# The RWKV-7 mixing stage of a two-layer encoder: five elementwise steps go to GpSimd, and VectorE's modulation products change places

## The reference

```
kk = heads(k * k_k);  kk = kk / max(norm(kk), 1e-12)
k  = k * (1 + (a - 1) * k_a)
y  = scan over t:  S = S*w_t + (S(-kk_t))(kk_t*a_t) + v_t k_t;  y_t = S r_t      (32 heads of 64)
y  = (y - mean) * rsqrt(var + eps) * ln_w + ln_b
y  = (y + sum(r*k*r_k) * v) * g        # bonus, gate
out = y @ w_o
```

## Time and profile before

| | |
|---|---|
| median of three runs | 2628.8 us |
| profiled execution | 2628.9 us |
| its span | 2627.3 us |
| TensorE busy in the span | 2526.0 us (96%) |
| VectorE | 1899.0 us (72%) |
| ScalarE | 1253.8 us (48%) |
| GpSimd | 46.5 us (2%) |
| granted TensorE clock, mean | 0.987 |

### The profile page before, as it was taken

The page is one execution under the profiler, slowest core; times in us unless marked ns, Lnnn a source line. Parts: engine busy times, 40 slices in busy tenths (PEclk is TensorE's granted clock), DMA queues, the critical chain, the costliest instruction groups (busy, mean ns, idle before and its releaser), DMA issues.

```text
span 2627.3 us, 53443 instructions
## 1 busy us (share of the span) xinstructions
PE 2526.0 (96%) x20124; PEld 2223.5 (85%) x20124; DVE 1899.0 (72%) x2596; ACT 1253.8 (48%) x1926; POOL 46.5 (2%) x85
## 2 busy tenths in 40 slices
PE   7999997998899999999999999999999999999998
PEld 6888877888788888888888888888888888888887
DVE  6868757887687777777777776677887655555556
ACT  2245555666445444444444554344454444444445
POOL 2000020000000000000000000000000000000000
PEclk9999999999999999999999999999999999999999
DMA  9998893445568888888887678567688566656653
GB/s 401 416 319 310 288 336 118 145 142 182 192 232 273 285 295 282 285 287 285 283 286 266 218 237 285 186 218 244 236 295 286 195 191 190 189 190 191 189 166 133
DMA packets 442249, 640.28 MB, mean 244 GB/s; under 512 B 21920, under 2 KB 402976, under 8 KB 420256
## 3 DMA queue, kind: packets, MB, share of 16 engines
q1 hardware_dynamic: 438400, 626.35, 70.1%
q0 software_dynamic: 3744, 12.59, 1.2%
HBM read 624.18 MB, written 14.68 MB: 243 GB/s over the span
## 4 chain that ended last, share of the span: by engine, by line
PE 68%; DVE 4%; ACT 1%; issue 1%; DMA 0%; DVEq 0%; ACTq 0%; SPq 0%
PE ps L1813 44%; PE ps L1817 22%; DVE ada_ring L1859 1%; DVE wlo L1797 1%; ACT whi L1792 0%; PE ps L1444 0%; PE ps L1438 0%; DMA ada_ring<-in_ada 0%; DVE st L1345 0%; PE ps L1477 0%; PE ps L1835 0%; DVE nt L132 0%; DVE lgf L1342 0%; PE ps L1469 0%; PE ps L1459 0%
## 5 line engine op out<-in xcount | busy, mean ns | idle before, releaser
L1797 DVE TENSOR_TENSOR wlo<-raw,whi 128x1024 fp32r<-128x1024 f32 (+1 forms) x736 | 865.6, 1191 | 436.5 <-ACT whi L1792 435.1
L1813 PE MATMUL ps<-act,whi 128*128 128x512 f32 x3528 | 1095.4, 392 | 0.8 <-DVE act L145 0.8
L1792 ACT ACTIVATE whi<-raw 128x1024 fp32r<-128x1024 f32 (+1 forms) x736 | 745.7, 1030 | 634.6 <-PE ps L1817 628.1
L1817 PEld LDWEIGHTS ps<-act,wlo 128*128 128x128 f32 x3528 | 662.6, 188 | 145.9
L1817 PE MATMUL ps<-act,wlo 128*128 128x256 f32 x3528 | 696.2, 279 | 0.0
L1813 PE MATMUL ps<-hid,whi 128*128 128x512 f32 x2176 | 685.4, 396 | 8.1 <-DVE wlo L1797 7.1
L1813 PEld LDWEIGHTS ps<-act,whi 128*128 128x128 f32 x3528 | 534.9, 188 | 1.4 <-DVE wlo L1797 1.0
L1817 PEld LDWEIGHTS ps<-hid,wlo 128*128 128x128 f32 x2176 | 411.3, 189 | 92.4
L1817 PE MATMUL ps<-hid,wlo 128*128 128x256 f32 x2176 | 433.4, 280 | 0.0
L1813 PEld LDWEIGHTS ps<-hid,whi 128*128 128x128 f32 x2176 | 331.5, 189 | 11.0 <-DVE wlo L1797 4.6
L1859 DVE SCALAR_TENSOR_TENSOR ada_ring<-ada_ring,silu 128x2048 f32<-128x2048 f32 x128 | 292.5, 2285 | 12.8 <-DMA ada_ring<-in_ada 12.8
(11 more groups left out here) (276 smaller groups left out, 2118.4 us busy)
## 6 DMA issues: line engine op xcount, KB each, us to landing
raw<-in_f_w SPq DMA_DIRECT2D x480, 512.0 KB, 4.5
ada_ring<-in_ada SPq DMA_DIRECT2D x144, 1024.0 KB, 7.7
raw<-in_a_w_rkv SPq DMA_DIRECT2D x96, 512.0 KB, 7.7
raw<-in_b_w_in SPq DMA_DIRECT2D x56, 512.0 KB, 3.8
ada_ring<-in_ada SPq DMA_DIRECT2D x48, 512.0 KB, 5.1
raw<-in_f_w SPq DMA_DIRECT2D x64, 384.0 KB, 3.9
first_ring<-in_ada SPq DMA_DIRECT2D x16, 1024.0 KB, 12.7
raw<-in_a_w_o SPq DMA_DIRECT2D x32, 512.0 KB, 6.8
```

The costliest lines, as they stand in the source:

```text
L1792: self.nc.scalar.activation(self.whi[:, u % SPL, 0:n], self.raw[:, u, 0:n], ACT.Copy).then_inc(self.s("hi_ready"), 1)
L1797: self.nc.vector.tensor_tensor(self.wlo[:, u % SPL, 0:n], self.raw[:, u, 0:n], self.whi[:, u % SPL, 0:n].bitcast(F32), SUB).then_inc(self. ...
L1813: self.nc.tensor.matmul(self.ps[0:c1 - c0, banks[b], :], hi[:, kk, c0:c1], src[:, k].rearrange("p a t -> p (a t)"), start=k == 0, stop=False)
L1817: last = self.nc.tensor.matmul(self.ps[0:c1 - c0, banks[b], T:2 * T], lo[:, kk, c0:c1], src[:, k, 0, :], start=False, stop=k == ktotal - 1)
```

## The change

GpSimd gets a program of its own in this stage: for iterations 0 to 6 it does the normalisation's product, weight and bias, bonus, gate and the low part, ten instructions over 128 x 256 elements an iteration (VectorE had eight, with the weight and bonus, and the bias and gate, in one instruction each). Iteration 7 stays on VectorE, which first waits for GpSimd's last. On VectorE `normed`, `gated_in`, `gated` and `remainder` go. Half 1 moves from the last chunk of C to N, in front of P2 (where half 2 was); halves 2 and 3 stand in front of W32, where the two y steps were; half 4 stays between W32 and W64; half 5 moves from there into chunk 2 of C; half 0 of the next iteration moves from chunk 1 to chunk 3, and `ada_sums` from chunk 0 to chunk 3. The order of SyncE, ScalarE and TensorE is not changed.

```diff
@@ VectorE stage_N
-                adas(i, 2)
+                adas(i, 1)
                 grow(i, "P2", 3, ADD, "P1")
...
                 grow(i, "P4", 3, ADD, "P3")
-                if post:
-                    normed(i - 1)
-                    gated_in(i - 1, 1 - q)
+                adas(i, 2, 3)
                 grow(i, "W32", 1, SUB, "P4")
                 if prep:
                     prep_c(i + 1, 1 - q)
-                adas(i, 3, 4)
-                if i >= 2:
-                    remainder(i - 2)
-                adas(i, 5)
+                adas(i, 4)
                 grow(i, "W64", 3, SUB, "W32")
@@ VectorE stage_C, in the loop over c
                         if prep:
                             for j in range(2):
                                 prep_d(i + 1, j)
-                        ada_sums(i)
                     if c in (1, 2) and prep:
                         prep_e(i + 1, c - 1)
-                    if prep and c % 2:
-                        adas(i + 1, c // 2)
-                    if c == 2 and post:
-                        gated(i - 1)
+                    if c == 2:
+                        adas(i, 5)
+                    if c == 3:
+                        ada_sums(i)
+                        if prep:
+                            adas(i + 1, 0)
@@ VectorE, before and after the loop
-            adas(0, 0, 1)
+            adas(0, 0)
...
-            remainder(L - 2)
...
+            past(dve, L - 1, "yg")
+            past(dve, L - 1, "y_lo")
             normed(L - 1)
@@ GpSimd, new
+            def finish(i, q):
+                for j in range(2):
+                    at(pool, i, "rsv", j)
+                    tt("yn", b["y"][:], b["yc"][:], b["yr"][:], MUL)
+                for j in range(2):
+                    at(pool, i, "yn", j)
+                    nc.gpsimd.tensor_scalar(b["y"][:], b["y"][:], col(i, PV_LNW, j), col(i, PV_LNB, j), MUL, ADD).then_inc(s("yw"), 1)
+                for j in range(2):
+                    at(pool, i, "yw", j)
+                    at(pool, i, "bon", j)
+                    tt("yb", b["y"][:], b["y"][:], b["bon"][q][:], ADD)
+                for j in range(2):
+                    at(pool, i, "yb", j)
+                    pool.wait_ge(s(f"g_loaded{j}"), i * 16 + 16)
+                    tt("yg", b["yo"][:], b["y"][:], b["g"][:], MUL)
+                for j in range(2):
+                    at(pool, i, "y_hi", j)
+                    tt("y_lo", self.hid_lo[:, m, :], R[j]["yo"][:].unsqueeze(1), self.hid_hi[:, m, :].bitcast(F32), SUB)
+            for i in range(L - 1):
+                finish(i, i % 2)
```

More of the change, by code:

```diff
@@ L2628, in tensor, with gpsimd, tt, col @@
                 self.multiply(u, UK, UK * u, KT, COLS, ((0, P), (P, 2 * P)), self.hid, (0, 1)).then_inc(self.s("unit_used"), 1)
-        return Stage(sync, scalar, vector, tensor)
+        def gpsimd(pool):
+            def tt(name, out, a, b, op):
+                nc.gpsimd.tensor_tensor(out, a, b, op).then_inc(s(name), 1)
+            def col(i, first, j):
+                return self.pv[:, bass.ds(i * 2 + (first + j), 1)]
+            def finish(i, q):
+                for j in range(2):
+                    b = R[j]
+                    at(pool, i, "rsv", j)
+                    tt("yn", b["y"][:], b["yc"][:], b["yr"][:], MUL)
+                for j in range(2):
+                    b = R[j]
+                    at(pool, i, "yn", j)
+                    nc.gpsimd.tensor_scalar(b["y"][:], b["y"][:], col(i, PV_LNW, j), col(i, PV_LNB, j), MUL, ADD).then_inc(s("yw"), 1)
+                for j in range(2):
+                    b = R[j]
+                    at(pool, i, "yw", j)
+                    at(pool, i, "bon", j)
+                    tt("yb", b["y"][:], b["y"][:], b["bon"][q][:], ADD)
+                for j in range(2):
+                    b = R[j]
+                    at(pool, i, "yb", j)
[3 more added lines that the diff above has]
+                    at(pool, i, "y_hi", j)
+                    m = bass.ds(i * 2 + j, 1)
+                    tt("y_lo", self.hid_lo[:, m, :], R[j]["yo"][:].unsqueeze(1), self.hid_hi[:, m, :].bitcast(F32), SUB)
+            for i in range(L - 1):
+                finish(i, i % 2)
+        stage = Stage(sync, scalar, vector, tensor)
+        stage.has_pool, stage.pool = True, gpsimd
+        return stage
     def ffn(self, layer, pieces, following):
```

## The result

The changed kernel takes 2644.9 us, the median of four runs (2642.0 to 2649.7), against 2628.7 before: the ratio is 1.0069, with a 95% interval of 1.0057 to 1.0081. It is slower by 16 us, more than twice the 7 us of the forecast: inside the stated range of 2619 to 2647, and above the 2631 to 2641 of the forecast itself. A second session gave 2642.8 (six runs, 2635.8 to 2649.6), ratio 1.0056 (1.0041 to 1.0071).

A forecast was written before the change was run, and what follows sets the result against it. Neither VectorE nor TensorE was full, so the order of single instructions decides. Gain, late loads and GpSimd waits, -12.5 + 16.2 + 3.6 = +7.3 us on 2628.9, gave 2636 us, range 2619 to 2647.

The forecast's parts named there:

- The likeliest case: N of iterations 1 to 6: the slip by late `in` outweighs the gain, 2636 us; chance 0.43.
- The signs named beforehand: ScalarE waits 3 to 4 us an iteration for `in`, its loads stand in one row, VectorE idles before P2, W32 to W64 shrinks.
- third rival: GpSimd instructions each hold VectorE up once through SBUF and XE's delay is not covered: 2644 us; chance 0.13.
- The slip of N: Late loads of `in` delay DX4 to W32 by 2.7 us (1.2 to 4.7) in iterations 1 to 6: 16.2 us.
- a dip of the clock: TensorE's clock dips in front of DX4 in place of the old dip: 0, or 4 us gained if none comes.
- L - 2.3: Chain slip in N, L being the time from last issue of `in` to landing: taken as 5.0, between 3.5 and 7.0.
- The gain: W32 to W64 1.26, chunk 1 to 2 0.82, less 0.4 and 0.1 later in C: 1.6 us an iteration, 12.5 together.
- GpSimd in the way: Halves 2 and 3 wait for GpSimd in N, making W32 0.6 us late in six iterations: 3.6 us.
- first rival: Loads of `in` land in time, L near 3.5, N slips 1.2 us: about 2622 us, faster; chance 0.24.
- Loads in time: Loads of `in` land with L below 4, N slips 1.2 us: about 2622 us, faster; chance 0.24.
- Nothing to be measured: L about 4.2, low gain before W64, GpSimd at half price, no dips: sum 0, 2629 us; chance 0.2.
- The shared way into SBUF: GpSimd and VectorE exclude each other in N and at the end of C: 8 us more, 2644 us; chance 0.13.

The follow-up runs named there:

- e1_order: The changed kernel with SyncE issuing the four loads of `in` ahead of modulation half 2 of the next iteration: 2616.6 us, ratio 0.9958.
- e2_late: The kernel before, with SyncE waiting for VectorE's U of chunk 3 ahead of modulation half 2 and the loads of `in`: 2662.3 us, ratio 1.0122.
- e5_warm_short: The changed kernel with 10 further matmuls of 256 columns in TensorE's standstill in N of iterations 1 to 7: 2643.7 us, ratio 1.0067.
- e6_chunk0: The changed kernel with half 5 in chunk 0 of C, the two sums in chunk 1, SyncE's order unchanged: 2612.7 us, ratio 0.9946.
- e3_gpsimd: The changed kernel with VectorE's modulation halves and sums back in their old places, y steps still on GpSimd: 2619.2 us, ratio 0.9971.

## Why the prediction was right, and where its sizes were off

**The cause.** The likeliest case was the one that came: SyncE's unchanged order makes the loads of `in` wait for half 5, ScalarE's `prep_v` waits for them, DX2 and the whole of N behind it. e1_order takes this away and turns the loss into a gain, and e2_late puts it into the old kernel and gets the loss. The signs named beforehand are there too. The size is another matter: the time is 4 us above the forecast's own 2641 and lies at the third rival's 2644, whose mechanism was not at work. That it is still inside the range is owed to the range's taking in that rival.

**The term that was too small.** The slip of N was put at 2.7 us and a dip of the clock at nothing, as it would only replace the old one. Two things were off. The landing took 5.5 to 6.0 us (5.0 was taken), which by the forecast's own formula, L - 2.3, gives 3.2 to 3.7; and TensorE's first product behind DX2 did come 3.2 to 3.8 us later (7.64 after XE at 517.48, before 3.94). The wait itself was thus forecast as it came. In the iteration without a dip, W32 stands 19.76 us after XE (601.00), before 15.92, so that 3.8 us are the late loads and what follows from them. And the dip does not cost the same in its new place. Before, it made an iteration some 0.75 us longer; in N it adds some 2. There TensorE stands still for 3.0 to 3.6 us and not 1.9, the clock falls before it starts again and stays at 0.50 for nearly 7 us (516.2 to 522.9), where before it was half as long (526.3 to 529.7), and in that time TensorE makes the products for DX4 and P2 one after another. That this is why it costs more is argued, not tested. With a dip W32 stands 22.06 us after XE: together 6.1 us where 2.7 stood, in iterations 2 to 6. Iteration 1, also counted, slipped only 1.7, as its DX2 was late before too. By e1_order the whole term is 29 us over the stage and not 16.

**The gain.** The forecast had 12.5 us less 3.6 for GpSimd in the way, that is 8.9; e1_order, the change without late loads, gained 0.42%, 11 us. That the two are near is in part chance. W32 to W64 fell by 2.35 us, and 1.38 of them passed on to the U of chunk 1 (1.26 was taken), because ScalarE's `prep_norm` was next, as foretold. Chunk 1 to 2 gave 0.75 (0.82 was taken). Chunk 2 to 3 lost 0.61 (0.4), and from the last U to XE 0.53 were lost (0.1). That leaves 1.0 us an iteration and not 1.6: 32.38 fell to 31.33. The rest of the 11 us are the old dips, 0.7 to 1.0 us in each of four iterations; with e1_order they went, and the iterations from the third on have a clock of 1.00. In the first rival's sum, the numbers given make 2621 us and not 2622.

**GpSimd in the way.** In N 0.6 us were taken. In the iteration shown none came through: half 3 took 1.74 us in place of 1.21, but TensorE's product for W32 was later still, 4.0 us behind P4 as before, in e1_order too. It isn't always so: in the iteration without a dip above, and in e5_warm_short's, half 2 took 1.85 us, half 3 1.73, VectorE went on to W32 without idling, and it started 0.23 us late. It did come through at the end of C, where nothing had been counted because `in` would be late: the two sums took 0.40 and 0.66 us beside the low parts (0.15 and 0.16 in e6_chunk0, away from them), and XE came 2.43 us after U in place of 1.90, in e1_order too. The price of a GpSimd instruction was right: 0.71 us alone (0.75 was taken), the weight and bias 0.56.

The Trainium skill (SBUF — State Buffer, "Who interferes with whom") has the two exclude each other for a whole instruction. The traces agree for GpSimd: its bonus additions beside halves 2 and 3 take 1.70 and 1.77 us, 0.71 in the last iteration where no half runs. VectorE is held up too, for somewhat less than an addition's 0.71 us: half 3 takes 0.53 us longer than 1.21, and half 2 0.64 longer in the iteration without a dip; half 2 of the iteration shown is not held up (1.22).

**The rivals.** Loads in time: no, 5.5 to 6.0 us and not under 4. Nothing to be measured: no, in both sessions the interval lies above 1. The shared way into SBUF as the main loss: no, e3_gpsimd has all ten instructions and is faster than before, and e2_late has none and the loss. Its 0.5 us at the end of C are real, and a part of why the gain is 1.0 us an iteration.

## What to carry to other kernels

When work moves to another place in an engine's order, look first at who waits for its completion count, above all at the queue that issues the loads: a load that stands behind it in program order moves with it, whether it needs it or not. Either the issue goes ahead of that wait or the work stays ahead of what released the load before; here the first was worth 29 us, and the second, with the sums moved as well, about as much (29 by the second session's time of the changed kernel, 32 by the first's). And before work is handed to a slower engine, try to place it in the waits of the first: with the order of e1_order the handing over gained nothing more.

## What the runs showed of the hardware that was not expected

- A standstill of TensorE of 3.0 to 3.8 us in N was mostly followed by a stretch at 1.2 GHz, and not always: in one execution of the changed kernel one iteration had a granted clock of 1.00, behind a standstill of 3.46 us, and the ones on either side 0.91 and 0.95; in the first profile one of 3.05 us was followed by nearly 7 us at 1.2 GHz. Before, standstills of 1.9 us in front of W64 were followed by it in four iterations and not in a fifth.
- About 100 products of 64 columns put into the loop as 200 instructions brought gaps of 2.9 and 1.5 us marked "issue" on TensorE; 20 instructions of 256 columns brought none of that size there.
- The last load of `in`, 256 KB, landed 5.5 to 6.4 us after its issue when four left in a row behind one of modulation weights (the changed kernel's two profiles, iterations 2 to 6), and 3.4 to 3.7 us when they left in two pairs (e1_order); in e6_chunk0, in two pairs too, it was 4.7 to 5.4, and why is not known.
- GpSimd's tensor_scalar with two scalars of a partition took 0.56 us over 128 x 256, less than its tensor_tensor (0.71).
